# Splitting the third pair of heads between VectorE and GpSimd, and four banks for the bias planes, in a two-block transformer kernel

## The reference, cut to what matters

```python
# first block, every layer, after attention:
q = (ht @ w_q).reshape(n_tok, 8, 256)                    # 8 heads
s1 = q[..., :128] @ sub_keys[0].T ; s2 = q[..., 128:] @ sub_keys[1].T   # 128 scores each
v1, i1 = top_k(s1, 16) ; v2, i2 = top_k(s2, 16)
cand = v1[:, None] + v2[None, :]                         # 16 x 16 sums
cidx = i1[:, None] * 128 + i2[None, :]
top, pos = top_k(cand, 16)
eidx = take_along_axis(cidx, pos)                        # the look-up: which expert
gate = softmax(top)
act = gelu(ht . expert_u[eidx]) ; y = sum(gate * act * expert_v[eidx])
# second block, attention: scores + bias, where for 8 heads and 256 x 256 positions
bias = table[t5_bucket(q_pos - k_pos)] ; visible = q_pos >= k_pos
```

## Time and profile before

| what | value |
|---|---|
| median of three runs | 3209.32 us (3207.16 to 3210.58) |
| the profiled execution | 3207.8 us, its span 3206.0 us |
| TensorE matmuls busy | 2986.2 us, 93% |
| VectorE busy | 1946.9 us, 61% |
| ScalarE busy | 1272.8 us, 40% |
| GpSimd busy | 270.6 us, 8% |
| mean granted TensorE clock | 0.964 of full speed |

### The profile page before, as it was taken

The page is one execution under the profiler, slowest core; times in us unless marked ns, Lnnn a source line. Parts: engine busy times, 40 slices in busy tenths (PEclk is TensorE's granted clock), DMA queues, the critical chain, the costliest instruction groups (busy, mean ns, idle before and its releaser), DMA issues.

```text
span 3206.0 us, 48637 instructions
## 1 busy us (share of the span) xinstructions
PE 2986.2 (93%) x17202; PEld 2541.3 (79%) x17202; DVE 1946.9 (61%) x3617; ACT 1272.8 (40%) x2038; POOL 270.6 (8%) x387
## 2 busy tenths in 40 slices
PE   8997899999999988879999999999998998999898
PEld 4674798999999865767999999988874987975697
DVE  4659866777777633996666666665542654643464
ACT  0235743444444321484444444434330433441233
POOL 0027600000000000580000000000000000000000
PEclk9898999999999998999999999999999999999999
DMA  8532156666666532204555666553333454323354
GB/s 304 203 111 79 47 188 204 229 227 231 228 229 228 193 137 79 93 1 158 189 187 186 194 196 192 192 180 151 127 132 119 157 184 166 123 109 126 131 184 144
DMA packets 130820, 524.26 MB, mean 164 GB/s; under 512 B 17997, under 2 KB 28109, under 8 KB 108041
## 3 DMA queue, kind: packets, MB, share of 16 engines
q1 hardware_dynamic: 120664, 508.13, 46.1%
q10 hardware_dynamic: 10034, 14.52, 1.3%
HBM read 519.44 MB, written 3.16 MB: 163 GB/s over the span
## 4 chain that ended last, share of the span: by engine, by line
PE 78%; issue 8%; DVE 6%; ACT 6%; DVEq 1%; ACTq 1%; DMA 0%; PEld 0%; POOL 0%; PEldq 0%; SPq 0%; POOLq 0%
PE prob_ps L1178 22%; PE acc L1190 22%; PE acc L862 7%; PE acc L802 4%; PE acc L823 3%; PE acc L847 3%; PE acc L1369 3%; PE acc L1384 3%; PE acc L1346 3%; ACT arena L1694 2%; PE turn_ps L955 2%; PE turn_ps L875 1%; PE acc L929 1%; ACT arena L1684 1%; ACT slab L1686 1%
## 5 line engine op out<-in xcount | busy, mean ns | idle before, releaser
L1178 PEld LDWEIGHTS prob_ps<-hTr,utr 128*128 128x128 f32 x5952 | 750.1, 192 | 33.7 <-issue 15.7
L1178 PE MATMUL prob_ps<-hTr,utr 128*128 128x256 f32 x5952 | 761.6, 285 | 8.6 <-DVE arena L2430 3.5
L1190 PE MATMUL acc<-vr,wtr 128*128 128x512 f32 x3000 | 728.1, 391 | 0.3 <-DVE vr L2407 0.2
L1190 PEld LDWEIGHTS acc<-vr,wtr 128*128 128x128 f32 x3000 | 547.9, 189 | 104.5 <-issue 0.8
L2407 DVE TENSOR_TENSOR vr<-slab,vr 128x1024 fp32r<-128x1024 f32 x250 | 306.2, 1225 | 411.9 <-ACT vr L1728 411.9
L1728 ACT CAST vr<-slab 128x1024 fp32r<-128x1024 f32 x250 | 262.4, 1050 | 581.4 <-PE acc L1190 578.4
L2382 DVE TENSOR_TENSOR utr<-slab,utr 128x1024 fp32r<-128x1024 f32 x248 | 301.9, 1218 | 14.8 <-ACT utr L1711 14.8
L1711 ACT CAST utr<-slab 128x1024 fp32r<-128x1024 f32 x248 | 259.3, 1046 | 9.8 <-DMA slab<-in_peer_u 5.0
L1964 POOL TENSOR_TENSOR small<-small 128x2 f32<-128x2 f32 (+3 forms) x18 | 20.8, 1154 | 2774.0 <-DVE small L2036 1477.3
L2623 DVE TENSOR_TENSOR slab_lo<-slab,w_hi 128x2048 fp32r<-128x2048 f32 x64 | 143.8, 2288 | 125.8 <-ACT w_hi L1936 125.8
L1718 ACT ACTIVATE arena<-prob_ps 128x256 f32<-128x256 f32 x248 | 95.4, 385 | 225.5 <-PE prob_ps L1178 225.5
(11 more groups left out here) (277 smaller groups left out, 3935.6 us busy)
## 6 DMA issues: line engine op xcount, KB each, us to landing
slab<-in_pack_b SPq DMA_DIRECT2D x132, 1024.0 KB, 4.9
slab<-in_peer_v SPq DMA_DIRECT2D x256, 512.0 KB, 3.5
slab<-in_peer_u SPq DMA_DIRECT2D x248, 512.0 KB, 4.6
arena<-in_pack_a SPq DMA_DIRECT2D x84, 512.0 KB, 4.9
slab<-in_pack_a SPq DMA_DIRECT2D x40, 1024.0 KB, 7.2
arena<-in_peer_u SPq DMA_DIRECT2D x4, 1024.0 KB, 13.1
slab<-in_pack_b SPq DMA_DIRECT2D x4, 832.0 KB, 6.0
arena<-in_pack_a SPq DMA_DIRECT2D x2, 1024.0 KB, 18.4
```

What stands on the lines that cost most here:

```text
L1178: ins = pe.matmul(prob_ps[:, m % 2, 0:S], utr[:, m % 2, uh, k * P:k * P + P], hTr[:, hh, k, :], start=(k == 0 and n == 0), stop=(k == KD - ...
L1190: ins = pe.matmul(y_ps[:, t, n, :], wtr[:, m % 2, wh, t * P:t * P + P], v[:, vh, n * 512:n * 512 + 512], start=first and k == 0, stop=last ...
```

## The change

It has two parts. In the first, `pick_keys` and `chosen` take a first tile and a number of tiles. VectorE looks up the third pair (index 2) for token tile 0 only, and GpSimd, after pairs 0 and 1, for token tile 1. `places_ready` gets a third signal in each layer (after best_of(5)), and TensorE waits for the third `picked` before it turns pairs0. The fourth pair stays whole on VectorE. In the second part, in the first layer only, the 8 bias planes go in turn to four banks, the two of `prob_ps` and the two of `turn_ps`, so that TensorE waits from the fifth plane on, for the plane four before.

```diff
@@ -278,8 +278,8 @@
         s_half, sk_half = Signal(sem("s_half"), a=4), Signal(sem("sk_half"), a=4)
         lists_ready = Signal(sem("lists_ready"), a=PH)
         cand_ready = Signal(sem("cand_ready"), a=PH)
-        places_ready = Signal(sem("places_ready"), a=POOLC)
-        picked = Signal(sem("picked"), a=POOLC)
+        places_ready = Signal(sem("places_ready"), a=POOLC + 1)
+        picked = Signal(sem("picked"), a=POOLC + 1)
         pairs_ready = Signal(sem("pairs_ready"), a=2)
         gated_rows = Signal(sem("gated_rows"), a=S // TOKG)
         plain_rows = Signal(sem("plain_rows"), a=S // TOKG)
@@ -513,6 +513,10 @@
         assert r5.at <= 8192
         t5_dram = nc.dram_tensor("t5_rows", [8, 512], F32).ap()
         bias_dram = nc.dram_tensor("bias_rows", [P, 8 * T * S], F32).ap()
+
+        def plane_bank(h):
+
+            return (prob_ps if h % 4 < 2 else turn_ps)[:, h % 2, :]
 
         def qpair(t, j):
 
@@ -1118,11 +1122,10 @@
                     pe.wait_ge(t5_skew, 16 * 16)
                     pe.wait_ge(t5_kept, 1)
                     for h in range(8):
-                        if h >= 2:
-                            pe.wait_ge(t5_done, h - 1)
-                        pe.matmul(prob_ps[:, h % 2, :], flip, skewed[:, h].rearrange("p t s -> p (t s)"),
-                                  start=True, stop=False)
-                        pe.matmul(prob_ps[:, h % 2, :], ident[:], causal_a, start=False, stop=True).then_inc(t5_flip, 1)
+                        if h >= 4:
+                            pe.wait_ge(t5_done, h - 3)
+                        pe.matmul(plane_bank(h), flip, skewed[:, h].rearrange("p t s -> p (t s)"), start=True, stop=False)
+                        pe.matmul(plane_bank(h), ident[:], causal_a, start=False, stop=True).then_inc(t5_flip, 1)
                     pe.wait_ge(t5_done, 8)
                     for s in (7, 8):
                         pe.wait_ge(bias_row_in, 16 * s)
@@ -1144,7 +1147,7 @@
                                         start=(k == 0), stop=(k == KD - 1))
                     ins.then_inc(early_full, 1)
                 pe.wait_ge(*pairs_ready.at("a", l, 1))
-                pe.wait_ge(*picked.at("a", l, POOLC))
+                pe.wait_ge(*picked.at("a", l, POOLC + 1))
                 turn("a", l, "pairs0", [pairs[:, i, t, :] for i in range(2) for t in range(T)])
                 pe.wait_ge(*pairs_ready.at("a", l, 2))
                 turn("a", l, "pairs1", [pairs[:, 2, t, :] for t in range(T)])
@@ -1412,54 +1415,56 @@
             copy(eng, dst, prob_ps[:, probs.buf(block, use), :]).then_inc(probs.free_sem(block, use), 1)
 
 
-        def chosen(eng, scratch, at, marks, op, table, dst):
+        def chosen(eng, scratch, at, marks, op, table, dst, tiles):
 
             on_pool = eng is nc.gpsimd
             n = 2 * PK
-            for t in range(T):
+            used = scratch[:, 0:tiles * n]
+            for t in range(tiles):
                 eng.tensor_tensor(scratch[:, t * n:t * n + n], spread(at[:, t], 2, PK), spread(marks, 1, n),
                                   ALU.subtract if on_pool else op)
             eng.drain()
             if on_pool:
-                eng.tensor_scalar(scratch, scratch, 0.0, None, op)
+                eng.tensor_scalar(used, used, 0.0, None, op)
                 eng.drain()
-            for t in range(T):
+            for t in range(tiles):
                 p4 = scratch[:, t * n:t * n + n].rearrange("p (h k) m -> p h k m", h=2)
                 eng.tensor_tensor(p4, p4, spread(table[:, t], 2, PK), ALU.mult)
             eng.drain()
-            p4 = scratch.rearrange("p (t k) m -> p t k m", t=T)
+            p4 = used.rearrange("p (t k) m -> p t k m", t=tiles)
             if on_pool:
                 for w in (8, 4, 2):
-                    eng.tensor_tensor(scratch[:, :, 0:w], scratch[:, :, 0:w], scratch[:, :, w:2 * w], ALU.add)
+                    eng.tensor_tensor(used[:, :, 0:w], used[:, :, 0:w], used[:, :, w:2 * w], ALU.add)
                     eng.drain()
                 return eng.tensor_tensor(dst, p4[:, :, :, 0], p4[:, :, :, 1], ALU.add)
             return eng.tensor_reduce(dst, p4, X, ALU.add)
 
-        def pick_keys(eng, scratch, tables, led, c):
-
-            ks = slice(2 * c * PK, (2 * c + 2) * PK)
-            at, part, step, where = (tables[:, i * T:i * T + T] for i in range(4))
-            led = led.rearrange("p (t h) k -> p t h k", t=T)
+        def pick_keys(eng, scratch, tables, led, c, first=0, tiles=T):
+
+            ks, ts = slice(2 * c * PK, (2 * c + 2) * PK), slice(first, first + tiles)
+            at, part, step, where = (tables[:, i * T:i * T + tiles] for i in range(4))
+            led = led.rearrange("p (t h) k -> p t h k", t=T)[:, 0:tiles]
             step = step.rearrange("p t (h k) -> p t h k", h=2)
-            keys = top_f.rearrange("p t (h f) k -> p t h f k", f=2)[:, :, 2 * c:2 * c + 2]
-            eng.tensor_copy(at, best_p.bitcast(U32)[:, :, ks])
-            for t in range(T):
+            keys = top_f.rearrange("p t (h f) k -> p t h f k", f=2)[:, ts, 2 * c:2 * c + 2]
+            row_of, col_of = pairs[:, 0, ts, ks], pairs[:, 1, ts, ks]
+            eng.tensor_copy(at, best_p.bitcast(U32)[:, ts, ks])
+            for t in range(tiles):
                 eng.tensor_tensor(led[:, t, :, 1:PK + 1], keys[:, t, :, 0], spread(row_part, 1, 2), ALU.add)
             eng.drain()
             eng.tensor_tensor(step, led[:, :, :, 1:PK + 1], led[:, :, :, 0:PK], ALU.subtract)
             eng.tensor_scalar(part, at, -1.0 / CANDS, None, ALU.mult)
             eng.drain()
-            chosen(eng, scratch, at, row_at, ALU.is_ge, step, where)
+            chosen(eng, scratch, at, row_at, ALU.is_ge, step, where, tiles)
             eng.drain()
             eng.tensor_tensor(part, part, where, ALU.add)
             eng.drain()
             eng.tensor_scalar(where, part, ROUND_MAGIC, None, ALU.add)
             eng.drain()
-            eng.tensor_scalar(pairs[:, 0, :, ks], where, ROUND_MAGIC, None, ALU.subtract)
+            eng.tensor_scalar(row_of, where, ROUND_MAGIC, None, ALU.subtract)
             eng.drain()
-            eng.tensor_tensor(part, pairs[:, 0, :, ks], part, ALU.subtract)
+            eng.tensor_tensor(part, row_of, part, ALU.subtract)
             eng.drain()
-            return chosen(eng, scratch, part, col_part, ALU.is_equal, keys[:, :, :, 1], pairs[:, 1, :, ks])
+            return chosen(eng, scratch, part, col_part, ALU.is_equal, keys[:, :, :, 1], col_of, tiles)
 
         @block_.scalar
         def _(act):
@@ -1654,7 +1659,7 @@
                         if h in (2, 4):
                             candidates(PH - 3 + h // 2)
                         act.wait_ge(t5_flip, h + 1)
-                        act.copy(skewed[:, h].rearrange("p t s -> p (t s)"), prob_ps[:, h % 2, :]).then_inc(t5_done, 1)
+                        act.copy(skewed[:, h].rearrange("p t s -> p (t s)"), plane_bank(h)).then_inc(t5_done, 1)
                     act.wait_ge(t5_done, 8)
                     load(t5_saved, bias_dram, skewed.rearrange("p h t s -> p (h t s)"))
                 else:
@@ -1974,6 +1979,10 @@
                     nc.gpsimd.sem_inc(passed["pool"], 1)
                     pick_keys(nc.gpsimd, pool_pick, pool_t, pool_lead, c).then_inc(picked.sem, 1)
                     nc.gpsimd.drain()
+                nc.gpsimd.wait_ge(*places_ready.at("a", l, POOLC + 1))
+                nc.gpsimd.sem_inc(passed["pool"], 1)
+                pick_keys(nc.gpsimd, pool_pick, pool_t, pool_lead, POOLC, 1, 1).then_inc(picked.sem, 1)
+                nc.gpsimd.drain()
 
                 nc.gpsimd.wait_ge(*turns.emptied_at("a", l, "pairs0"))
                 nc.gpsimd.sem_inc(passed["pool"], 1)
@@ -2331,7 +2340,7 @@
                     dve.wait_ge(*cand_ready.at("a", l, h + 1))
                     dve.sem_inc(passed["dve"], 1)
                     ins = best16([(cand[:, t, h], best[:, t, h], bu[:, t, h * PK:(h + 1) * PK]) for t in range(T)])
-                    if h % 2 and h < 2 * POOLC:
+                    if h % 2 and h < 2 * POOLC + 2:
                         ins.then_inc(places_ready.sem, 1)
 
                 lists(0)
@@ -2339,7 +2348,7 @@
                     lists(h)
                     best_of(h - 1)
                 dve.drain()
-                pick_keys(dve, pick, pick_t, lead, 2)
+                pick_keys(dve, pick, pick_t, lead, POOLC, 0, 1)
                 best_of(PH - 1)
                 dve.drain()
 
```

## The result

The changed kernel is slower. Its first six launches have a median of 3226.53 us (3219.98 to 3231.71), those of the kernel before 3209.15 us; the ratio is 1.0042, with a 95% interval of 1.0024 to 1.0061. The profiled execution took 3227.85 us, with a span of 3226.0 us, 20.0 us longer than before.

The account below looks back on a forecast made before the run. VectorE's last look-up was taken to set the gate stage's start. POOL's half, ending last, added +4.7 and +1.9 us, the banks nothing: 3209.3 + 6.6 = 3216 us as a median, range 3210.5 to 3221.

Parts of the forecast that it names:

- Who ends last: Look-up before the gate stage: POOL's half ends last, at 290.0 and 1367.2 us, delaying the layers by 4.7 and 1.9 us.
- POOL's half: POOL's added one-tile look-up: 13.1 us busy plus 3.1 us of gaps, 16.2 us, 63% of a whole one.
- gaps and fixed parts also halve: First rival, POOL's added look-up: needs only 13 us, together +0.4 us, 3208 to 3210 us; chance 0.12.
- VectorE's chain sets the gates: Second rival, start of the gate stage: POOL is not last, 9.1 us faster, 3200 us; chance 0.06.
- third rival: POOL's added look-up: heavier contention, 2.3 us more in each layer, +11.2 us in all, 3220.5 us; chance 0.12.
- VectorE's saving: VectorE's halved third look-up: last look-up ends 5.4 and 6.4 us earlier, less 1 to 2 us for its fourth pair's overlap.
- The four banks: First layer's bias planes: copied by about 261.9 us, conditioning pieces end near 278.3; costed at nothing, hidden by the look-up.
- all behind it moves with it: From the gate stage on: VectorE's last look-up sets its start, so the shift of the last look-up goes through whole.

Follow-up runs that it names:

- e3: Changed kernel, but VectorE looks up the whole third pair and POOL's third piece repeats one tile of the second pair; median 3221.9 us, ratio 1.0040.
- e4: Changed kernel with POOL's third piece cut to two small copies, leaving out the third pair's token tile 1; median 3203.5 us, ratio 0.9977.
- e12: Kernel before with four banks, first layer's low half of hT on POOL, second layer's look-ups split by heads; median 3214.8 us, ratio 1.0019.
- e2: Kernel before with only the four banks added; median 3209.7 us, ratio 1.0004.
- e1: Changed kernel with its bias planes back in two banks, so the look-up split alone; median 3221.9 us, ratio 1.0037.
- e11: The changed kernel itself, launched six more times; median 3222.1 us, ratio 1.0046 against the kernel before.
- e9: Kernel before with eight extra compares on POOL between its second look-up and its signal, first layer only; median 3226.2 us, ratio 1.0056.
- e10: Changed kernel split by heads: POOL looks up head 0, then 1 and 2, then 3 and 4, VectorE the rest; median 3212.7 us, ratio 1.0009.
- e7: Kernel before with the four banks and, in the first layer, the low half of hT made by POOL; median 3208.6 us, ratio 1.0000.
- e6: Changed kernel with the look-up split in the second layer only; median 3214.6 us, ratio 1.0018.
- e5: Changed kernel with the look-up split in the first layer only; median 3218.3 us, ratio 1.0023.
- e8: Kernel before with five extra compares on POOL between its second look-up and its signal, first layer only; median 3214.9 us, ratio 1.0011.

## Why the prediction was right in sign and too small

**Who ends last: right.** The step that made POOL's half the bound held in both layers, and e3 and e4 show it from both sides. POOL's last add came at 291.16, forecast 290.0; the second layer's mark rose by 2.0 us, forecast 1.9. The sum of the marks is +7.4 us, forecast +6.6. The rival in which gaps and fixed parts also halve fell: the half was 18.5 us and not 13. The one in which VectorE's chain sets the gates fell with it.

**POOL's half: mis-sized, and offset.** The term was 16.2 us and measured 18.54 and 18.25. The four small instructions at its start, for which I had 1.0 us of work, lie beside VectorE's two-input instructions of its fourth look-up, and so does the first tree (2.54 us for 256, 128 and 64 elements where the second takes 1.75):

```profile
272.62 0.37 POOL L1450 CAST arena<-arena 128x32 f32<-128x32 uint32 x1 [0.25 <-issue]
272.94 0.69 POOL L1452 TENSOR_TENSOR small<-arena,small 128x32 f32<-128x32 f32 x1
273.78 0.61 POOL L1454 TENSOR_TENSOR arena<-small 128x32 f32<-128x32 f32 x1
274.45 0.64 POOL L1455 TENSOR_SCALAR arena<-arena 128x32 f32<-128x32 f32 x1
...
279.71 2.54 POOL L1437 TENSOR_TENSOR arena<-arena 128x256 f32<-128x256 f32 x3
...
289.03 1.75 POOL L1437 TENSOR_TENSOR arena<-arena 128x256 f32<-128x256 f32 x3
```

Against it, the second look-up took 1.6 us less than I let it (26.56 for 28.19), by the contention that VectorE's shorter look-up gave back. I had set what is given back and what is new equal, with 2 us a layer either way; new were 2.3 us (18.54 for 16.2) in the first layer, so they differ by 0.7 us. The third rival, 2.3 us more on POOL and nothing given back, had the first half of that right. In e12 a VectorE tensor_scalar took 4.47 us beside a POOL instruction of 4.49 that had started 0.07 us before it. The Trainium skill's page SBUF — State Buffer, "Who interferes with whom", says that between a VectorE instruction in a 2-port mode and GpSimd whoever issues first gets the shared pair of ports for the whole instruction and the other fully blocks, and that tensor_scalar can enter such a mode. The trace agrees in the times; it doesn't show the mode. So VectorE can be the loser, where the prediction's use of the rule only held up POOL.

**VectorE's saving: mis-sized, at no cost.** I put its third look-up at about 7 us beside POOL in the first layer; it took 8.03, so the change freed 4.4 us and not 5.4. Its fourth took 2.3 us more than alone, where I had 1 to 2, and the subtraction ahead of it 1.28 us, beside a tree of POOL's (269.26 to 271.93), where it took 0.42:

```profile
269.51 1.28 DVE L2357 TENSOR_TENSOR arena<-arena 128x256 f32<-128x256 f32 x1
270.72 0.72 DVE L1450 CAST arena<-arena 128x64 f32<-128x64 uint32 x1
```

So its last reduce ended at 283.40, where I had about 281, and 1.9 us earlier than before. It cost nothing: VectorE then waited 7.90 us for pairs1, inside the 6 to 9 us forecast.

**The four banks: right.** Nothing, in e2 and in e1. The last plane was copied at 262.14 (forecast 261.9); TensorE's first conditioning piece then ran partly at half clock (8.47 us for 7.03), so the pieces ended at 280.8 and not 278.3, inside the bound given and hidden all the same.

**The step that failed: "all behind it moves with it".** I took the shift at the start of the gate stage as the whole price, since nothing behind it would be ready earlier. The edited stretches do sum to 7.8 us of the 20.0. But the schedule behind did not move rigidly: the second layer's attention took 61.5 us for 55.7, in every launch profiled, with more of it at half clock. That is 5.8 us, as much as the first layer's delay itself; the stretch ahead of it gave back 0.8 to 1.0 us. The marks' 7.4 us alone lies under the intervals of all three runs of the split (from 7.7, 10.6 and 8.0 us on, for the changed kernel, e11 and e1), so the local delay is not the whole price. Marks and attention together are +13.1 to +13.5 us for the three (column A + B), and the ratios of e1, of the changed kernel and of e11 say 11.9, 13.5 and 14.8. The first six launches' median, 17.4 us over before, is some 4 us more than their own ratio and than the median of e11's six; the last layer's stretch, which differs from launch to launch by up to 6.5 us, is where I would look for that, and no run shows it of the medians. No rival of mine had a longer attention in it; 3209.3 + 13.5 = 3222.8 is over the top of the range already.

**What the attention's length goes with.** It is not the size or the sign of the delay: e4 is 5 us early, e9 8 us late and e10 0.4 us early at the first expert product, and all three take 64.1 to 64.2 us. The profiles together show something closer. Between the two layers TensorE waits for the other engines, and in every profile the granted clock falls to the lower level there, some 65 us ahead of the attention stretch. Where this fall lies in the work, counted from the first expert product, sorts the kernels. The falls and the times at 1.2 GHz are from the traces' record of the granted clock:

| profiles | fall after the first expert product, us | time at 1.2 GHz in the attention, us | attention, us | stretch ahead of it, us |
|---|---|---|---|---|
| before (four), e2, e7 | 744.3 to 744.5 | 6.8 | 55.4 to 55.8 | 809.3 to 809.5 |
| e6 | 744.2 | 17.1 | 59.6 | 809.3 |
| changed (three), e1, e5, e8, e12 | 742.9 to 743.9 | 20.5 | 61.4 to 61.5 | 808.4 to 808.9 |
| e3, e4, e9, e10 | 741.5 to 741.7 | 34.1 | 64.1 to 64.2 | 807.2 to 807.4 |

```profile
1188.08:1247.73 59.65, 51.61 (x203) 31.67 (x200) 23.95 (x54) 15.18 (x49) 0.00 (x0) 0.86 0.13 48
```

```profile
1185.64:1249.83 64.19, 58.88 (x204) 37.31 (x200) 24.25 (x54) 15.18 (x49) 0.00 (x0) 0.73 0.11 44
```

These are the attention windows of e6 and of e10. The fall did not move with the work: in the changed kernel it came at 1127.1 us for 1123.3, 3.8 us later, where the work had moved by 5.3 us. The earlier it comes in the work, the longer the attention runs at 1.2 GHz, and that takes in e10. e6 is told from e2 by 0.1 us only, so there it is a description and no explanation. No run moved the place of the fall by itself, so this order is read off and not shown as the cause.

**What stays open.** The stretch's length is no price in full. A + B agrees with the ratio to 1.5 us in the changed kernel, e1, e2, e6, e7 and e11, but is 2.6 to 3.7 us too high in e5, e9, e10 and e12, 4.9 in e4 and 6.5 in e3 and e8. Part of this is in the table: the stretch ahead of the attention is 2 us shorter in e3, e4, e9 and e10 and up to 1 us shorter in the other delayed ones. The rest wasn't traced. The ratio is of 5 to 12 launches and the stretch of one, and in e3 and e9 that one began its look-ups 5 us earlier than the others (VectorE's third at 253.50 and 253.58, for 257.3 to 261.7), so their stretches needn't be those of their medians. It wasn't tried to keep TensorE busy through the attention.

## What to carry to other kernels

Before work is moved to an idle engine, price it there from its own rows with the gaps kept: half of a look-up cost GpSimd 18.5 us, over 70% of a whole one, because the gaps at the drains (2.9 us for 3.1) and the small instructions don't halve, and it freed only 4.4 us of VectorE. Two engines that hold each other up, as VectorE and GpSimd did here, don't add up; look for what the other is doing in the same microseconds. And where later stages leave TensorE work in fragments, a delay of 5 us brought as much again elsewhere here: compare equal stretches of work in both traces, by the same instructions, before the whole difference is put down to the edit, and profile a second launch before a stretch is put down to the kernel.

## What the runs showed of the hardware that was not expected

A VectorE tensor_scalar of 64 elements took 4.47 us beside a GpSimd tensor_tensor of 2048 (e12), where it takes 0.20 us. The same unedited work, second-layer attention to out projection, took from 55.4 to 64.2 us over the profiles of this case, by how long TensorE was granted only its lower level in it (6.8 to 34.1 us), and that went in order with where in the work an earlier fall of the clock lay. And a gain was cut as a loss was enlarged: e4 gained 11.2 us in its marks and 7.4 us by its ratio.
